# A three-part transformer kernel on one core: later constants, an earlier flush of deferred steps, and output columns begun before their last rows exist

## The reference, cut to what matters

```python
def first_block(...):                      # first layer, once
    h = rms_norm(x, norm_mix)
    # h @ w_in: q,k,v of branch A (4 heads, differential attention), of branch B
    # (4 heads x 3 dilated window groups), and q of branch C (attends to mem)
    ck, cv = split(rms_norm(mem, mem_norm) @ w_mem_kv)      # 256 memory tokens
    x = x + sum(sigmoid(h @ w_gate + b_gate) * branches, 2) @ w_out
    x = x + (silu(h2 @ w_ffn_gate) * (h2 @ w_ffn_up)) @ w_ffn_down

for l in range(2):                         # recurrent layers
    x = x + 0.5 * swiglu(rmsnorm(x, ffn1_norm[l]), ...)
    q_a, f_a, i_a, g_a, u_b = split(rmsnorm(x, mix_norm[l]) @ w_in[l])
    o_a = hgrn2_mixer(q_a, f_a, i_a, g_a, lb, norm_g)       # 4 heads: norm, gain, silu gate
    o_b = multiscale_pool(u_b, pool_w, pool_scale)          # 4 groups
    x = x + concatenate([o_a, o_b], -1) @ w_out[l]
    x = x + mem_cross_attention(rmsnorm(x, xa_norm[l]), mem_n, wq, wkv, wo)  # 4 heads of 256
    x = x + 0.5 * swiglu(rmsnorm(x, ffn2_norm[l]), ...)
```

## Time and profile before

| | us |
|---|---|
| median of 3 runs | 3343.69 (3342.83 to 3343.94) |
| the profiled execution's own time | 3344.81 |
| its span | 3342.9 |
| PE busy in the span | 3254.8 (97%) |
| DVE busy | 1718.9 (51%) |
| ACT busy | 1119.5 (33%) |
| PE's mean granted clock, 1.0 being 2.4 GHz | 0.994 |

### The profile page before, as it was taken

How to read it: one execution, slowest core, us unless ns; L and a number is a source line. 1 busy time by engine, 2 the same in 40 slices (tenths; PEclk the granted TensorE clock), 3 DMA queues, 4 the chain that set the end, 5 groups by cost and what they waited for, 6 DMA issues and landing times.

```text
span 3342.9 us, 39813 instructions
## 1 busy us (share of the span) xinstructions
PE 3254.8 (97%) x14944; PEld 2662.5 (80%) x14944; DVE 1718.9 (51%) x2483; ACT 1119.5 (33%) x1771; POOL 0.2 (0%) x4
## 2 busy tenths in 40 slices
PE   9999999999999999999999999999999999999998
PEld 7777777778888888888876888888888878688887
DVE  5664445565443545346754554344543676554542
ACT  4654545532222222232333322232222333332221
POOL 0000000000000000000000000000000000000000
PEclk9999999999999999999999999999999999999999
DMA  4223323232322222331321222322223223122222
GB/s 141 99 78 101 97 74 114 70 114 94 100 94 95 99 95 94 101 111 63 101 95 45 98 97 94 100 95 94 98 97 110 82 76 108 57 89 95 99 95 88
DMA packets 88536, 313.33 MB, mean 94 GB/s; under 512 B 9952, under 2 KB 10336, under 8 KB 87904
## 3 DMA queue, kind: packets, MB, share of 16 engines
q1 hardware_dynamic: 82224, 294.69, 26.2%
q10 hardware_dynamic: 6192, 16.97, 1.6%
HBM read 309.52 MB, written 2.10 MB: 93 GB/s over the span
## 4 chain that ended last, share of the span: by engine, by line
PE 91%; DVE 4%; ACT 3%; issue 2%; DMA 1%; SPq 0%; DVEq 0%; ACTq 0%
PE ps L931 28%; PE ps L933 28%; PE ps L932 27%; PE ps L1201 1%; PE ps L1116 1%; ACT stage_sq L1341 1%; PE ps L1105 1%; PE ps L1148 1%; PE ps L1006 1%; ACT whi L1247 0%; DMA x_res<-in_x 0%; PE ps L1231 0%; PE ps L1094 0%; PE ps L1152 0%; PE ps L1131 0%
## 5 line engine op out<-in xcount | busy, mean ns | idle before, releaser
L931 PE MATMUL ps<-x_hi,whi 128*128 128x512 f32 x2400 | 944.8, 394 | 0.0
L933 PE MATMUL ps<-x_hi,wlo 128*128 128x512 f32 x2400 | 935.5, 390 | 0.0
L932 PE MATMUL ps<-x_lo,whi 128*128 128x512 f32 x2400 | 934.9, 390 | 0.0
L1247 ACT ACTIVATE whi<-raw 128x1024 fp32r<-128x1024 f32 (+1 forms) x555 | 583.2, 1054 | 998.5 <-DMA raw<-in_weights 994.2
L1485 DVE TENSOR_TENSOR wlo<-raw,whi 128x1024 fp32r<-128x1024 f32 x553 | 674.5, 1222 | 418.3 <-ACT whi L1247 409.8
L931 PEld LDWEIGHTS ps<-x_hi,whi 128*128 128x128 f32 x2400 | 451.1, 188 | 97.6 <-issue 5.4
L933 PEld LDWEIGHTS ps<-x_hi,wlo 128*128 128x128 f32 x2400 | 451.0, 188 | 94.6
L932 PEld LDWEIGHTS ps<-x_lo,whi 128*128 128x128 f32 x2400 | 451.1, 188 | 94.3 <-issue 2.4
L933 PE MATMUL ps<-h_hi,wlo 128*128 128x512 f32 x880 | 342.4, 389 | 0.0
L931 PE MATMUL ps<-h_hi,whi 128*128 128x512 f32 x880 | 342.4, 389 | 0.0
L932 PE MATMUL ps<-h_lo,whi 128*128 128x512 f32 x880 | 342.4, 389 | 0.0
(11 more groups left out here) (278 smaller groups left out, 3342.6 us busy)
## 6 DMA issues: line engine op xcount, KB each, us to landing
raw<-in_weights SPq DMA_DIRECT2D x553, 512.0 KB, 3.2
bias<-in_biasB ACTq DMA_DIRECT2D x16, 384.0 KB, 3.2
bias<-in_biasA ACTq DMA_DIRECT2D x16, 256.0 KB, 3.2
mem_raw<-in_mem ACTq DMA_DIRECT2D x3, 1024.0 KB, 7.4
x_res<-in_x SPq DMA_DIRECT2D x8, 256.0 KB, 7.1
x_res<-in_x ACTq DMA_DIRECT2D x1, 2048.0 KB, 9.3
out_x<-x_res SPq DMA_DIRECT2D x8, 256.0 KB, 2.0
raw<-in_weights SPq DMA_DIRECT2D x2, 256.0 KB, 4.4
```

Source lines behind the costliest of these rows:

```text
L931: pe.matmul(out, hi, xhi, start=start, stop=False)
L932: pe.matmul(out, hi, xlo, start=False, stop=False)
L933: return pe.matmul(out, lo, xhi, start=False, stop=stop)
L1247: return act.activation(out, in_, ACT.Copy, scale=scale)
```

## The change

Deferred steps: `part` flushes at its beginning, and `factors` (the step `gnorm`) goes on a second list, `soon`, which is run at the end of the same part or job. `turns` takes two columns only while four are left, otherwise one, always slot `O` first.

```diff
         def part(u):
+            self.flush()
             unit = len(self.units)
...
-            self.flush()
+            self.flush_soon()
...
         def roots():
             self.step("ginv", **a)
-            self.defer(factors)
+            self.soon.append(factors)
...
-            for slot in ("O", "T0") if isinstance(a["g"], tuple) else ("T0", "O"):
-                if turned:
-                    self.step("gturn", c=turned.pop(0), slot=slot, **a)
+            for slot in ("O", "T0")[:2 if len(turned) > 3 else 1]:
+                self.step("gturn", c=turned.pop(0), slot=slot, **a)
```

In `job`, `flush_soon` follows `flush`. `spread` puts the first piece into slot 1 and the last into the last slot:

```diff
+    places = [1 + round(k * (slots - 1) / max(len(work) - 1, 1)) for k in range(len(work))]
...
-        upto = len(work) * min(state[1], slots) // slots
-        while state[0] < upto:
+        while state[0] < len(work) and places[state[0]] <= state[1]:
```

First layer: `setup` moves behind the fourth key part. The memory is loaded into a place that is free once branch B's head 2 is done, five gate columns of branch B are computed inside the attention of its head 3 (before: two), `memfresh` runs in two lots of four behind the first two pairs, and one gate column stands between the keys and values:

```diff
-    step("setup")
     for m in range(4):
         step("refresh", n=0, m=m, gain="norm_mix", entered=True)
     a_keys[1]()
...
     a_keys[3]()
+    step("setup")
     step("masks")
...
-    b_work = [..., b_parts[37:] + [lambda m=m: gate_chunk(1, m, ("GT", m)) for m in range(2)]]
+    b_work = [...,
+              b_parts[37:38] + [memload] + b_parts[38:] + [lambda m=m: gate_b(m) for m in range(5)]]
...
-    memload()
-    pair_b(0)
-    for k, go in enumerate((lambda: gate_b(2), lambda: gate_b(3), lambda: pair_b(1), lambda: gate_b(4))):
-        go()
-        memparts[2 * k]()
-        memparts[2 * k + 1]()
+    for jj in range(2):
+        pair_b(jj)
+        for go in memparts[4 * jj:4 * jj + 4]:
+            go()
     memsum()
-    gate_b(5)
...
-    for go in c_keys + c_values:
+    for go in c_keys + [lambda: gate_b(5)] + c_values:
```

```diff
-                        copy(OAH[:, role["dst"][1], :], src, gain_of(role["gain"])).then_inc(*sig("ohi", role["id"]))
+                        whole = AOS[role["dst"][1] % 2].rearrange("p t c d -> p (t c d)")
+                        copy(whole, src, gain_of(role["gain"])).then_inc(*sig("hq", role["id"]))
+                        act.wait_ge(*on("hq", role["id"]))
+                        copy(OAH[:, role["dst"][1], :], whole).then_inc(*sig("ohi", role["id"]))
...
-                        free["S1"] = ("pt", i)
+                        free["S1"] = ("pt", (i, "far"))
```

Recurrent layers: the norm, transpose and gate of pair 0's first head move ahead of its second head. `first` is the triple (`ginv`; `gnorm`; `gturn` into `O`, `hgate`, `split`):

```diff
-        def between():
-            hprep(1, s.njobs - 1)
+        def between(first):
+            evacuated = s.njobs - 1
+            first[0]()
+            first[1]()
+            hprep(1, evacuated)
             pool_job(3)
+            first[2]()
         first, second = heads_out(0, between)
         second_pair[6]()
+        second[0]()
         pool_rest(3)
-        first[0]()
+        second[1]()
```

```diff
+        begun = [s.column_parts("w_out_2", l, m, mix_rows, 6, **mixed(m)) for m in range(3)]
+        begun[0][0]()
         second[2]()
         s.drain()
+        begun[1][0]()
+        begun[2][0]()
...
-        for go in queries[:4]:
+        for go in queries[:2]:
             go()
...
+               queries[2:] + [start for start, _ in begun], places=(2, 5, 9, 13, 17, 21, 28, 30, 32))
```

More of the change, by code:

```diff
@@ L163, in part, with column_parts, start, finish @@
                     self.norm_group(a)
-            self.flush()
-        return [lambda u=u: part(u) for u in range(4)]
+            self.flush_soon()
+        return [lambda u=u: part(u) for u in range(4)]
+    def column_parts(self, name, l, column, rows, cut, /, **a):
+        at = {}
+        def start():
+            at["t0"], at["j"] = len(self.units) * UT, self.njobs
+            self.njobs += 1
+            self.unit(name, l, [(k, column) for k in rows])
+            self.open_units(at["t0"] // UT + min(AHEAD, RING - 1 - a["m"]))
+            self.settle()
+            self.step("job", j=at["j"], tile0=at["t0"], nk=DC, k0=0, k1=cut, rows=rows, **a)
+            norms, self.norms = self.norms, []
+            for kind, n in norms:
+                self.step(kind, n=n)
+            self.flush()
+            self.flush_soon()
+        def finish():
+            self.open_units(at["t0"] // UT + AHEAD)
+            self.step("job", j=at["j"], tile0=at["t0"], nk=DC, k0=cut, k1=DC, rows=rows, **a)
+            self.step("evac", j=at["j"], tile0=at["t0"], nk=DC, rows=rows, **a)
+            self.flush()
+            self.flush_soon()
+            return at["j"]
+        return start, finish
     def norm_group(self, a):
@@ L188, in norm_group, with flush_soon @@
         self.defer(roots)
+    def flush_soon(self):
+        soon, self.soon = self.soon, []
+        for go in soon:
+            go()
     def flush(self):
@@ L195, in drain @@
     def drain(self):
-        while self.later:
+        while self.later or self.soon:
             self.flush()
+            self.flush_soon()
     def settle(self):
@@ L296, in build_schedule, with placed, fill, attend @@
     ntiles = 0
-    def attend(tiles, work, after_pv=None):
+    def placed(work, places):
+        left, state = list(zip(places, work)), [0]
+        def fill():
+            state[0] += 1
+            while left and left[0][0] <= state[0]:
+                left.pop(0)[1]()
+        return fill
+    def attend(tiles, work, after_pv=None, places=None):
         nonlocal ntiles
@@ L303, in attend @@
         before = ntiles - 1
-        fill = spread(work, 20 if kind == "X" else 2 * len(tiles))
+        fill = placed(work, places) if places else spread(work, 2 * len(tiles))
         due = []
@@ L525, in heads_out @@
             first = norm_of(0)
-            between()
+            between(first)
             step("hout", l=l, pr=pr, hh=1)
@@ L575, in build_schedule, with between @@
         kv = keys(6, 7) + value_parts(4) + keys(0, 1) + value_parts(0) + keys(2, 3, 4, 5)
-        levels(1, [[first[1], second_pair[7], first[2], second[0]], [kv[0], second[1], kv[1], second[2]], kv[2:3], kv[3:4],
+        levels(1, [[second_pair[7], second[2]], kv[0:2], kv[2:3], kv[3:4],
                    [lambda: step("hsilu", l=l, pr=1, need=("gnorm", (("H", l, 1), 0)))] + kv[4:6],
                    kv[6:7], kv[7:8], kv[8:9], kv[9:11], kv[11:12]])
-        first, second = heads_out(1, kv[12])
-        first[0]()
+        def between(first):
+            kv[12]()
+            first[0]()
+        first, second = heads_out(1, between)
         kv[13]()
@@ L584, in build_schedule, with mixed @@
         kv[14]()
-        first[2]()
         second[1]()
         kv[15]()
+        first[2]()
+        norm += 1
+        mix_rows = (4, 5, 6, 7, 0, 1, 2, 3)
+        def mixed(m):
+            return dict(rhs="mix", n=T, evac="resid", m=m, c=1.0,
+                        need={k: [("olo", ("M", l, k))] for k in range(DC)} if m == 0 else {})
+        begun = [s.column_parts("w_out_2", l, m, mix_rows, 6, **mixed(m)) for m in range(3)]
+        begun[0][0]()
         second[2]()
         s.drain()
-        norm += 1
+        begun[1][0]()
+        begun[2][0]()
         for m in range(DC):
-            need = {k: [("olo", ("M", l, k))] for k in range(DC)} if m == 0 else {}
-            j = column("w_out_2", l, m, rows=(4, 5, 6, 7, 0, 1, 2, 3), rhs="mix", n=T, evac="resid", m=m, c=1.0, need=need)
+            j = begun[m][1]() if m < 3 else column("w_out_2", l, m, rows=mix_rows, **mixed(m))
             step("refresh", n=norm, m=m, gain=f"xa_norm_2_{l}", need=("evac", j))
@@ L874, in program, with turn_slot, turned_in @@
         TURN = {"T0": PS[:, 2, :], "O": O}
+        def turn_slot(a):
+            return "T1" if a["kind"] == "C" and a["i"] % 2 else "T0"
+        def turned_in(a):
+            return PS[:, 3 if turn_slot(a) == "T1" else 2, :]
         def probs(a):
@@ L1007, in _ @@
                     mm.then_inc(*sig("gt", (a["g"], c)))
[L1008 to L1009 removed]
+                    free[a["slot"]] = (("hgated", a["g"][1:]) if role["dst"][0] == "MIX" else ("hq", role["id"]))
                 elif kind == "job":
```

65 lines of the change are left out of this document (35 added, 30 removed).

## The result

The changed kernel takes 3360.3 us (median of four runs, 3355.7 to 3363.5), the kernel before, run beside it, 3343.3. The ratio is 1.0049 with a 95% interval from 1.0037 to 1.0062: 17 us slower, where 18 us faster was forecast. The time lies outside the range of 3308 to 3340.

The account below looks back on a forecast made before the run. PE, busy 97% of the span, was taken as the bound, so only its pauses and low clock could be won. The terms sum to -17.7 us, from 3343.7 to 3326; own bounds 3315 to 3337, range 3308 to 3340.

Parts of the forecast that it names:

- Deferred steps in branch A: Branch A's attention: PE's pauses at the turns' transposes and for `oa_lo` go, 5.7 us left of 12.2: -6.5 us.
- Branch B: Branch B's attention: the next turn's copy comes sooner, the last head gets eight pieces, one us left: -14.8 us.
- Rival (c): Branch B's cover fails: ACT's root and table load meet the next exponential, its 13 us stay; 3339 us, chance 0.11.
- Heads of pair 0: Recurrent layers: second head's `hout` waits 9.9 us for the first head's gate on DVE; +7.5 a layer, +15.0 us.
- rival (e): Heads: table switches dearer than their rows, ACT standing 1.3 us more at each of two; 3331 us, chance 0.03.
- Rival (d): Clock stays low through pair 1's levels after the heads' pause, up to 24 us more a layer; 3374, chance 0.06.
- Setup: Kernel start: moved `setup` saves an early pause, but PE waits for DVE's first product at L952; sum +5.3 us.
- Memory: Between branch B's output and the memory's norm: less cover, PE waits 3.7 us at L964, clock 1.7: +5.4 us.
- Branch C: Branch C's attention: of 7.5 us idle, small waits remain at two turns and a value product: -4.6 us.
- Recurrent layers: Both layers: pauses and low clock go at pair 1's heads with `w_out_2` (-10.2 us) and attention to the memory (-7.3).
- (a): Only the heads' pause comes true, the waits at L952 and L964 do not; 3313 us, chance 0.12.
- (b): None of the three waits (heads, L952, L964) appears, as if gate and sums shared no queue; 3289 us, chance 0.06.

Follow-up runs that it names:

- the fourth experiment: The changed kernel with the heads of pair 0 in their old order (first head's norm, transpose and gate behind the second head): 3346.5 us, ratio 1.0005.
- the ninth experiment: The kernel before with only the recurrent layers' edits (columns begun early, two queries ahead of the scores, places by hand): 3334.5 us, ratio 0.9974.
- three parts back: The changed kernel with the place of `setup`, the deferred steps' timing and slots, and the order of pair 0's heads as before: 3321.7 us, ratio 0.9937.
- the second experiment: The changed kernel with the old timing and slots of the deferred steps (flush at a part's end, two columns per flush): 3340.0 us, ratio 0.9989.

## Why the prediction was wrong

**Deferred steps in branch A: this step failed.** It said that the pauses go because "a part of 5.4 us now lies behind each `gturn`, and `O` needs one copy". It counted what lies behind a transpose on PE and not what lies ahead of its operands on the other queues. Measured, L1078 waits 14.9 us for copies (6.1, 4.3, 4.5) and the stage takes 12.8 us more, where 6.5 less was forecast. Of the 12.8 us, 10.5 went with timing and slots undone (shown). "Needs one copy" was true; the copy of 0.67 us stands behind the exponentials of the score after it. For the memory keys the prediction had the right rule: the transpose is the next thing on PE, so the pause stays. It wasn't asked where else that holds. In the rows above it holds where two parts follow each other with no score between, and where `gnorm` stands in DVE's queue at a part's end.

**Branch B: the same step failed.** It counted the 1.5 us of ACT's table load and root as moved out of the way. They were moved ahead of a weight unit, and `gnorm` behind it: 7.2 us of waits for `stage` in this stretch. The stage gives -3.9 in place of -14.8. With the old timing and the new `spread` it is -8. The rest of the forecast gain is not there in any run, so the count "one us left" was wrong beyond the timing: in that run PE still stands idle for 6.9 us of the stage, with these as the largest waits of the turns ("issue" is time in which PE waited for nothing that the profile shows):

```profile
PE ps L1188 <- issue: 3.1, 7, 0.8
PE ps L1188 <- DVE small L1784: 1.5, 1, 1.5
```

Rival (c) came nearest. It named the place (ACT's root and the exponentials meet) and priced it as a gain not made, 3339. What it lacked was a loss: such a meeting can cost more than the pause that it replaces.

**Heads of pair 0: right.** The pause is 9.2 us (forecast 9.9, between 5.2 and 9.9), the price 6.7 and 7.0 us a layer (forecast 7.5), taken away by the fourth experiment. One term of the chain did not come: the prediction let ACT load a table ahead of the root. The trace has no load there (the root runs at 1601.92, the only load follows it), and from pair 0's first `hout` to the first sigmoid it takes 6.6 us, 0.7 more than before in the second layer, not 1.5 more; that is about the gap between 9.9 and 9.2. The term of the Trainium skill (ScalarE: Activation LUTs, section What ACT_TABLE_LOAD costs) would have made it 12.6 us. After the change too, the load at 1602.15 ends at 1603.43 and the sigmoid begins at 1603.44: no drain in the row, and rival (e) falls. Rival (d) as well: the clock was at the lower level behind the pause (first row, 0.55), and at the higher one in the levels (second row), in the profile after. The levels of pair 1 from first to last take 57.2 us in the kernel before, not the 48 that this rival counts; it changes nothing in the verdict.

```profile
1610.00:1620.00 10.00, 5.64 (x25) 5.48 (x26) 5.40 (x13) 0.83 (x2) 0.00 (x0) 0.55 0.01 2
1625.00:1681.00 56.00, 56.00 (x364) 50.77 (x363) 43.58 (x62) 17.38 (x18) 0.00 (x0) 1.00 0.37 123
```

**Setup: the wait right, the price not as a term that adds.** Branch A begins 5.2 us later (forecast 5.3), with the wait of 5.0 at L1024. That the numbers agree so closely is in part luck: the same opening code puts branch A's beginning anywhere between 97.6 and 101.8 us in four profiles. With the old timing the late `setup` costs some 5 us, under the new one it gives only 1 back when undone.

**Memory: right.** PE waits 2.1 us at L1036 and 1.2 at the first product with the memory, 3.3 for a forecast 3.7. The stage gives +2.9 for +5.4; the forecast added 1.7 of clock, and the granted clock was 1.00 here. **Branch C:** -2.4 for -4.6; with the old timing it is -4.2, so what is missing there went with the deferred steps too.

**Recurrent layers: the sum close, its make-up not.** -15.6 for -17.5 in the profiles. But 2.5 and 3.3 us of the forecast were clock, won in the first layer alone. In the ninth experiment such a stretch at the lower level turned up elsewhere, so the edit is worth 3.5 to 4.8 us a layer.

Rivals (a) and (b) fall: all three waits came (9.2 twice, 5.0, 2.1). The kernel with three parts back comes near the forecast of 3326 in time, but without the heads' pause that is in it, so it doesn't bear the forecast out. The prediction's own bounds of 3315 to 3337 don't follow from the 9 and 8 us that it gives for them (3309 to 3334); the measured time lies outside both.

Still open: how the -8 of branch B under the old timing divide; no run separates the cover in the last head from the moved columns there.

## What to carry to other kernels

When a step is deferred, price both ends: what its consumer has as cover, and what stands ahead of the step on the queue that carries it out, in list order, down to the 0.7 us copy that frees a slot. A pair of steps put round a block of other work (here root and norm round a weight unit) puts that block on their chain. And a whole that loses may hold parts that win: here three of the parts cost 37 us, and the rest was worth 21.

## What was not expected of the hardware

The lower clock is not the property of a place, which an edit there can earn back. The same 1218 matmuls took 257.2 and 251.5 us in one execution (clock 0.97 and 1.00), and unchanged code at 575 to 585 us ran at 0.84 in one kernel and 1.00 in the other. Over whole spans the mean clock went roughly with PE's idle time: 0.991 at 99 us with the change, 0.994 at 88 before, 0.996 at 76 with three parts back, though the second experiment reads 0.992 at 88. Two causes did not add: undone alone they gave 7 and -2 us, together 20.
